# Second part of an expert pair's rows gathered as half rows on 128 partitions and turned by identity products on two array quadrants

## The reference

```python
def _hier_moe(h, w_rg, b_rg, w_re, b_re, w_gate, w_up, w_down):
    t = h.reshape(-1, D_MODEL)
    ... # gate: the two weights of a token's experts, zero elsewhere
    for g in range(N_EGROUPS):
        a = jnp.einsum('td,edf->tef', t, w_gate[g])
        up = jnp.einsum('td,edf->tef', t, w_up[g])
        act = jax.nn.silu(a) * up * gate[:, g, :, None]
        out = out + jnp.einsum('tef,efd->td', act, w_down[g])
    return out.reshape(shp)
```

## Time and profile before

| | us |
|---|---|
| median of 3 runs | 1453.1 |
| lowest, highest | 1444.98, 1454.42 |
| profiled execution | 1448.88 |
| its span in the trace | 1447.1 |
| PE busy in it | 1339.0 |
| span of one pair of experts | 18.81 |

### The profile page before, as it was taken

How to read it: one execution, slowest core, us unless ns; L and a number is a source line. 1 busy time by engine, 2 the same in 40 slices (tenths; PEclk the granted TensorE clock), 3 DMA queues, 4 the chain that set the end, 5 groups by cost and what they waited for, 6 DMA issues and landing times.

```text
span 1447.1 us, 23251 instructions
## 1 busy us (share of the span) xinstructions
PE 1339.0 (93%) x9114; PEld 1039.5 (72%) x9114; DVE 563.5 (39%) x814; ACT 379.3 (26%) x573; POOL 458.9 (32%) x379
## 2 busy tenths in 40 slices
PE   6999999998989898999989899999987999999990
PEld 5999999998759876976887699995474444444430
DVE  3454440015555754864585560011153111111115
ACT  4212123443333423533242351210121111111102
POOL 5244433334341532543163254340001222222110
PEclk8899999999998999999899999999966999999995
DMA  5123223247106303510541222336711999999925
GB/s 142 45 73 87 72 73 87 73 138 201 45 1 167 87 14 91 133 43 0 144 109 43 65 73 73 88 117 206 318 53 37 378 366 356 373 362 371 380 103 204
DMA packets 179364, 209.54 MB, mean 145 GB/s; under 512 B 13019, under 2 KB 154459, under 8 KB 170959
## 3 DMA queue, kind: packets, MB, share of 16 engines
q1 hardware_dynamic: 168010, 188.05, 39.4%
q10 hardware_dynamic: 4126, 10.83, 2.2%
q0 software_dynamic: 7168, 9.81, 1.9%
HBM read 196.73 MB, written 32.15 MB: 158 GB/s over the span
## 4 chain that ended last, share of the span: by engine, by line
PE 74%; DVE 12%; issue 5%; DMA 4%; ACT 3%; SPq 1%; DVEq 1%; POOL 0%; ACTq 0%; POOLq 0%
PE acc L578 34%; PE pT L921 8%; PE acc L796 5%; DVE area L1120 4%; PE pS L934 4%; PE acc L960 4%; DMA ring<-in_w_in 3%; PE pY L728 2%; PE pS L968 2%; PE pS L672 2%; PE acc L897 1%; PE acc L694 1%; PE pO L610 1%; DVE big L1191 1%; PE pY L904 1%
## 5 line engine op out<-in xcount | busy, mean ns | idle before, releaser
L578 PE MATMUL acc<-h_parts,ring_parts 128*128 128x328 f32 (+1 forms) x3840 | 550.6, 305 | 9.4 <-POOL ring_parts L1691 8.6
L578 PEld LDWEIGHTS acc<-h_parts,ring_parts 128*128 128x128 f32 x3840 | 536.9, 192 | 22.4 <-issue 21.6
L1691 POOL TENSOR_TENSOR ring_parts<-ring,ring_parts 128x1024 fp32r<-128x1024 f32 x104 | 262.8, 2527 | 427.4 <-ACT ring_parts L1438 427.3
L1438 ACT ACTIVATE ring_parts<-ring 128x1024 fp32r<-128x1024 f32 x104 | 110.0, 1058 | 359.9 <-PE acc L578 326.9
L921 PE MATMUL pT<-area,big 128*64 128x512 f32 x384 | 116.2, 612 | 0.3 <-ACT big L1620 0.3
L578 PE MATMUL acc<-u_parts,ring_parts 128*128 128x264 f32 (+1 forms) x640 | 109.5, 299 | 0.0
L1120 DVE SCALAR_TENSOR_TENSOR area<-area,xvec 128x616 f32<-128x616 f32 x72 | 94.2, 1309 | 10.5 <-DVE area L1118 0.6
L578 PEld LDWEIGHTS acc<-u_parts,ring_parts 128*128 128x128 f32 x640 | 96.4, 188 | 0.0
L921 PEld LDWEIGHTS pT<-area,big 128*64 128x64 f32 x384 | 35.2, 140 | 79.2 <-issue 79.2
L578 PE MATMUL acc<-area_parts,ring_parts 128*128 128x264 f32 (+1 forms) x512 | 91.2, 299 | 0.0
L578 PEld LDWEIGHTS acc<-area_parts,ring_parts 128*128 128x128 f32 x512 | 78.4, 188 | 0.0
(11 more groups left out here) (320 smaller groups left out, 1727.2 us busy)
## 6 DMA issues: line engine op xcount, KB each, us to landing
ring<-in_w_in SPq DMA_DIRECT2D x80, 512.0 KB, 4.0
area<-in_w_gate SPq DMA_DIRECT2D x24, 1024.0 KB, 6.6
area<-in_w_up SPq DMA_DIRECT2D x24, 1024.0 KB, 9.3
area<-in_w_down SPq DMA_DIRECT2D x24, 1024.0 KB, 10.6
area<-in_state_ssm SPq DMA_DIRECT2D x16, 512.0 KB, 7.1
out<-area SPq DMA_DIRECT2D x16, 512.0 KB, 6.4
ring<-in_w_ssd_out SPq DMA_DIRECT2D x16, 512.0 KB, 3.6
ring<-in_w_gate SPq DMA_DIRECT2D x8, 1024.0 KB, 11.2
```

Of the source, the lines that this page charges most:

```text
L578: m = nc.tensor.matmul(acc[a][:, h, 0:n], w[s][:, k, :], x[:, k, h * HALF:h * HALF + n], start=first and k == 0 and w is w_hi and x is hi, ...
L1438: a_.activation(w_hi[b % 2], w_raw[b % 2], ACT.Copy).then_inc(hi_done, 1)
L1691: gp.tensor_tensor(w_lo[b % 2], w_raw[b % 2], w_hi[b % 2].bitcast(F32), ALU.subtract).then_inc(lo_done, 1)
```

## The change

The second part of a pair is gathered from `h2_half`, the same table seen as 1184 half rows of 2 KB: partitions 0 to 63 get the first halves of the 64 rows, partitions 64 to 127 the second halves. `xe_over` is then 128 partitions by 512 columns in place of 64 by 1024. `gid_over` has 128 entries, made as `sid_over` is (double, add 0 or 1, cap), which takes one more DVE instruction. `turn_over` turns each half on its own quadrant of the array: the first half's 64 rows and 64 features on the quadrant of rows and columns 0 to 63, the second's on rows and columns 64 to 127, with `matmul` by the identity in place of `transpose`. What lands in `pY` is the same as before.

```diff
-        xe_main, xe_over = xe[0:2], [x[0:2 * OVER, :] for x in xe[2:4]]
+        xe_main, xe_over = xe[0:2], [x[:, 0:512] for x in xe[2:4]]
...
+        h2_half = h2_rows.rearrange("r (h c) -> (r h) c", h=2)
...
                 for k in range(8):
-                    m = nc.tensor.transpose(pY[:, k * 2 * OVER:(k + 1) * 2 * OVER], xe_over[p % 2][:, k:D:8],
-                                            ident[0:2 * OVER, 0:2 * OVER])
+                    for h in (slice(0, 2 * OVER), slice(2 * OVER, 4 * OVER)):
+                        m = nc.tensor.matmul(pY[h, k * 2 * OVER:(k + 1) * 2 * OVER], xe_over[p % 2][h, k:512:8], ident[h, h],
+                                             start=True, stop=True)
                 m.then_inc(m_tr, 1)
...
-            v.tensor_scalar(gid_over[:, :], pT[0:2 * OVER, 0:PAIRS], float(NO_TOKEN), gather_cap[0:2 * OVER, :], ALU.add, ALU.min
-                            ).then_inc(r_ids, 1)
+            link(v.tensor_scalar(gid_f, pT[:, 0:PAIRS], 2.0, half, ALU.mult, ALU.add))
+            v.tensor_scalar(gid_over[:, :], gid_f, half_gather, None, ALU.min).then_inc(r_ids, 1)
...
+            link(gp.memset(half_gather[0:1, :], float(2 * T - 2)))
...
-                for x, index in ((xe_main, gid_main), (xe_over, gid_over)):
-                    pool.indirect_dma_start(x[p % 2], None, h2_rows[:, :],
+                for x, index, rows, n in ((xe_main, gid_main, h2_rows, T), (xe_over, gid_over, h2_half, 2 * T)):
+                    pool.indirect_dma_start(x[p % 2], None, rows[:, :],
```

More of the change, by code:

```diff
@@ L201, in build @@
         tokback, b = carve(b, [2, TILES], big, B5)
-        caps, b = carve(b, [4], big, B5)
+        caps, b = carve(b, [5], big, B5)
         sid_f, b = carve(b, [PAIRS], big, B5)
+        gid_f, b = carve(b, [PAIRS], big, B5)
         places, b = carve(b, [CAP], big, B5)
@@ L211, in build @@
         gate, gate_later = sb("gate", [P, 2, TILES]), sb("gate_later", [P, 2, TILES])
-        gid_main, gid_over = sb("gid_main", [2 * MAIN, PAIRS], I32), sb("gid_over", [2 * OVER, PAIRS], I32)
+        gid_main, gid_over = sb("gid_main", [2 * MAIN, PAIRS], I32), sb("gid_over", [4 * OVER, PAIRS], I32)
         sid_main, sid_over = sb("sid_main", [2 * MAIN, PAIRS], I32), sb("sid_over", [4 * OVER, PAIRS], I32)
@@ L1312, in _ @@
             dve.wait_ge(r_idtr, 1)
-            gather_cap, empty, half, half_cap = (caps[:, n:n + 1] for n in range(4))
+            gather_cap, empty, half, half_cap, half_gather = (caps[:, n:n + 1] for n in range(5))
             v.tensor_scalar(gid_main[:, :], pS[:, 0:PAIRS], float(NO_TOKEN), gather_cap, ALU.add, ALU.min)
-            v.tensor_scalar(gid_over[:, :], pT[0:2 * OVER, 0:PAIRS], float(NO_TOKEN), gather_cap[0:2 * OVER, :], ALU.add, ALU.min
-                            ).then_inc(r_ids, 1)
+            link(v.tensor_scalar(gid_f, pT[:, 0:PAIRS], 2.0, half, ALU.mult, ALU.add))
+            v.tensor_scalar(gid_over[:, :], gid_f, half_gather, None, ALU.min).then_inc(r_ids, 1)
             v.tensor_scalar(sid_main[:, :], pS[:, PAIRS:2 * PAIRS], float(NO_TOKEN), empty, ALU.add, ALU.min)
@@ L1813, in _ @@
                          allow_small_or_imprecise_dtypes=True))
-            gather_cap, empty, half, half_cap = (caps[:, n:n + 1] for n in range(4))
+            gather_cap, empty, half, half_cap, half_gather = (caps[:, n:n + 1] for n in range(5))
             link(gp.memset(half[0:2 * OVER, :], float(2 * NO_TOKEN)))
             link(gp.memset(half[2 * OVER:4 * OVER, :], float(2 * NO_TOKEN + 1)))
-            for cap_ in (gather_cap, empty, half_cap):
+            for cap_ in (gather_cap, empty, half_cap, half_gather):
                 x = gp.memset(cap_, float(3 * NO_TOKEN))
@@ L1834, in gather @@
             def gather(p):
-                for x, index in ((xe_main, gid_main), (xe_over, gid_over)):
-                    pool.indirect_dma_start(x[p % 2], None, h2_rows[:, :],
+                for x, index, rows, n in ((xe_main, gid_main, h2_rows, T), (xe_over, gid_over, h2_half, 2 * T)):
+                    pool.indirect_dma_start(x[p % 2], None, rows[:, :],
                                             bass.IndirectOffsetOnAxis(ap=index[:, p:p + 1], axis=0),
-                                            bounds_check=T - 1, oob_is_err=False).then_inc(xe_in[p % 2], 16)
+                                            bounds_check=n - 1, oob_is_err=False).then_inc(xe_in[p % 2], 16)
             gather(0)
```

## The result

| | before | after |
|---|---|---|
| median, us (5 runs each) | 1451.5 | 1462.84 |
| lowest, highest | 1444.98, 1454.42 | 1456.85, 1466.81 |
| profiled execution, its span | 1448.88, 1447.1 | 1462.84, 1461.1 |

The ratio is 1.0092, with a 95% interval of 1.0068 to 1.0117: slower by 11 us. The median lies inside the 1% band, whose edge the interval reaches over, and inside the range, but the loss is six times what the likeliest case gave.

What follows compares the result with a forecast made beforehand. PE was taken to bound the experts' stage. 1448.88 + 1.2 (loop) + 0.7 (start) = 1450.8 us profiled, or 1453.1 + 1.9 = 1455 on the scale of medians; range 1447 to 1470.

Steps and rivals of the forecast that it cites:

- the likeliest case: Whole kernel: quadrants work together at near 60 ns a step, giving 1455 us; chance 0.68.
- PE sets the pace, and a shorter turn gives nothing: Experts' loop: PE bounds it; the old turn only fills a wait for DVE, so shortening it gains nothing.
- The room: Between L942 and L950 in each pair: 1.04 us that the turn can fill before it costs time.
- The quadrants work side by side: Second part's turn: products on both quadrants run at once, so 32 instructions take 16 steps.
- rival serial: Second part's turn: quadrants alternate, 32 single steps, +16 to +19 us, 1469 to 1472; chance 0.17.
- Twice the instructions for a product: Second part's turn: an f32 product is recorded twice, a transpose once, so 32 instructions against 8.
- The price of a step: New turn in the loop: 57 to 63 ns for each of 16 steps, 108 ns at most.
- a floor that L851 hides: New turn: a sign of a wrong forecast, a minimum cost for loading 64 columns; no size given.
- dear slots: New turn: quadrants run together but a 64-column instruction costs 108 ns, +12 and +2 us, 1467; chance 0.05.
- Changes of tiling: End of the new turn, going from 64x64 to another array shape: 0.11 us added.
- The start: Start of the experts' stage: DVE +0.25, POOL +0.06 and first turn +0.37, sum +0.7 us, from +0.3 to +2.5.
- The gather, POOL's queue, ACT's copy: Experts' loop: twice as many gather entries, POOL's extra 0.06 us and ACT's copy of pY cost nothing.

Runs made afterwards that it cites:

- one-of-eight run: The kernel before with only 1 of the 8 transposes of the second part's turn, the other 7 left out: ratio 0.9986.
- gather_alone: The changed kernel with its half-row gather, but a turn of 8 transposes (64 rows by 128 columns) of the first halves only: ratio 1.0002.
- in-turn run: The changed kernel with the turn's two loops exchanged, all products on one quadrant and then all on the other: 1502.98 us.
- full-width pair: Two runs: the kernel before with 8 identity products of 128 columns for its transposes, taking every eighth column (1508.18 us) or neighbouring columns (1464.07 us).
- full_products: The kernel before with its 8 transposes replaced by 8 identity products of the same size, 64 rows by 128 strided columns: 1508.18 us.
- before_moved: The kernel before with only PE's order changed: L942 right behind turn_main, L950 between the two halves of L960: ratio 1.0002.
- column_halves: The kernel before with whole rows on 64 partitions, turned by 16 identity products on two column halves instead of transposes: ratio 1.0122.

## Why the prediction was right and wrong

**PE sets the pace, and a shorter turn gives nothing.** Right. A pair grew by what the turn grew, and the one-of-eight run shows the cover. The room was slightly larger than the 1.04 us read from the earlier trace rows, since L950 was itself waiting for DVE there: with transposes at 120 ns (`gather_alone`) the last of them starts 0.07 us later and L950's place does not move.

**The quadrants work side by side.** Right, and in one PSUM bank: starts within 10 ns, and one quadrant alone takes as long as two. The Trainium skill ("TensorEngine Tiling (Array Packing)", Restrictions and Gotchas) says that different row tiles cannot access one PSUM bank at the same time. Here two of them did, in different partitions of the bank, with starts within 10 ns and no cost. The rival serial would have been a turn of 3.56 us, as the in-turn run has it, dearer than the 1.9 to 2.1 that the prediction gave it. The prediction's signs for serial in the profile (a turn of about 1.9 us, a pair of 19.7 or more) came true without it; only the starts tell the two apart.

**Twice the instructions for a product.** Right: x32 for 16 products. The full-width pair shows it by itself: x16 for 8 products, and 1.93 us with neighbouring columns.

**The price of a step.** This is where the prediction failed. The prediction took 57 to 63 ns, from L851 at the half clock, and called 108 ns, from L728, the upper bound with the reason that "half the columns cannot cost more". It measured 120 ns. Both rows have neighbouring columns as stationary operand; the turn takes every eighth, and there a product's step costs 1.87 ns a column at either clock, against 0.9 at the full clock and 1.7 at the half. With neighbouring columns the step is 58 ns, so the row from L851 was scaled rightly and was the right row but for the stride. The term is +1.02 us a pair in place of +0.08, over the 15 turns of the loop +15.3 us in place of +1.2. The prediction did name "a floor that L851 hides" as a sign of being wrong, but not where it would come from.

The trace of the kernel before held a warning. It has two transposes of one shape, 64 rows by 128 stationary columns, L904 with every eighth column and L950 with neighbouring ones, and their weight loads differ (ns min/median/max of one load). The third line has eight transposes near the start of the program, on 80 rows by 128 neighbouring columns:

```profile
L904 PEld LDWEIGHTS pY<-ident,big x128: 182/202/203, 1104.4 to 1384.8; 64*128 64x128 f32 x128
L950 PEld LDWEIGHTS pO<-ident,big x32: 133/137/140, 1121.7 to 1402.9; 64*128 64x128 f32 x32
...
21.53 0.77 PE L602 MATMUL acc<-ident,area 80*128 80x80 f32 x8 [1.92 <-DVE area L1013]
```

A load of every eighth column is recorded at 202 ns against 137, and the eight of L602 take 0.77 us where those of L904 take 1.09. Neither was a test of the stride alone, but both were there to be asked about it.

In the prediction's cases this is the rival called dear slots, with a chance of 0.05, at 120 ns in place of 108: 1467 forecast, 1462.84 measured. The likeliest case, with 0.68, was wrong in its mechanism, and the range held the time only because it had to take in serial, a rival that did not come. That is luck.

**Changes of tiling.** The new one at the turn's end did not show: with neighbouring columns L953 starts 0.15 us after the last product, and after the last transpose of `gather_alone`, where the tiling stays, it is 0.15 too. With neighbouring columns the turn is 1.08 us, 16 x 58 = 0.93 and 0.15 for its first and last gap, so +0.04 us a pair, where +0.08 was foreseen.

**The start.** +0.7 foreseen, +1.04 measured: 0.38 for index and gather (0.31 foreseen) and 0.66 for the turn (0.37 foreseen). The turn's 16 steps of 114 ns, 1.82 us, were held against 1.14 for the eight transposes; but that 1.14 takes in the last one's end, 0.31 us after its start, and the steps do not. Measured to its end the new turn is 2.19 us. The clock gave back 2.4 us in the first pair, which the prediction did not have and which is not shown to come from the change.

**The gather, POOL's queue, ACT's copy.** Right: nothing in the loop.

**What stays open.** Why 8 bytes are near and 16 are far was not tried. What the stride costs a transpose was not tried either: the loads above are recorded 65 ns longer with it, and no run turned the second part by transposes of neighbouring columns. The clock's fall in the runs on one quadrant and in `full_products` was seen, not tested by an experiment of its own, and so was its earlier or later rise at the start of the stage.

## What to carry to other kernels

Before a piece of PE's work is shortened, look at the place in the trace where it is absent, such as a loop's last round: if the next instruction starts no sooner there, the piece is free and only its growth counts. A price for a matmul is good only for the same mode, number of instructions and step between the stationary columns: an f32 turn by products has two recorded instructions where a transpose has one, and its step doubles again when the columns lie 16 or 32 bytes apart. To shorten such a turn, fill the array's rows with more tokens for each transpose, and first move whatever it was covering.

## What was not expected of the hardware

- The step of an f32 product's instructions with 64 stationary columns, 16 or 32 bytes from one to the next, is 120 ns, and with 128 columns 32 bytes apart 240, at granted clocks of 1.00 and 0.50 alike. With 64 columns 8 bytes apart it is 60, with neighbouring ones 58, and 107 for both at the half clock; with 128 neighbouring ones 112 and 213. Transposes of 64 rows by 128 columns take 110 ns at 32 bytes and 120 at 16, at either clock too.
- The granted clock fell to 1.2 GHz with PE never idle: after 2.06 us on one quadrant alone in 5 of 14 pairs and after 3.56 us on one quadrant at a time in 7 of 14, at 1.7 us each time, and with 3.94 us of products on 64 rows in 10 of 14, at 1.7 us and more. With both quadrants in use for 2.07 us, or both column halves on 64 rows for 2.08, it stayed at 2.4 GHz.
- At the start of the stage the full clock came at different times: the first pair of the `before_moved` run took 1.2 us more than its later ones, that of the kernel before 2.8, that of `column_halves` 2.6 and that of the changed kernel 0.4, with first turns of 1.1 us in the first two and 2.1 in the last two.
